# First block of a two-block transformer kernel: convolution rows stacked through HBM, two heads per root, router and its root with tokens on partitions, gates spread in one pass

## What is computed

```
h = rms_norm(x); z = h @ w_in            # 1024 -> 2304: a_val, a_gate, p_in, q, k, v
conv:  u = a_val * sigmoid(a_gate); 31-tap causal depthwise convolution of 256 channels;
       layer_norm, silu, @ w_pw (256 x 256)
pool:  causal means over 2, 4, 8, 16 tokens of 4 x 64 channels, minus the input, @ w_pool
attention: 4 heads, two score maps each, p0 - lam * p1, rms_norm of each head's output
x = x + concat(conv, pool, attention) @ w_out
hf = rms_norm(x); group logits hf @ wg (4) and expert logits hf @ we (16);
       best group, its 4 experts, top 2 of them -> gates (256 x 16)
y = sum over e of (silu(hf @ w_gate[e]) * (hf @ w_up[e]) * gates[:, e]) @ w_down[e]   # 16 experts, 256 wide
x = x + y
```

## Time and profile before

| | |
|---|---|
| median of 3 runs | 1813.24 us (1812.34 to 1813.38) |
| profiled execution, its own time | 1815.85 us |
| its span, first to last instruction | 1814.0 us |
| PE matmuls, share of the span | 1741.5 us, 96% |
| VectorE, ScalarE, GpSimd busy | 1196.5, 807.3, 271.7 us |
| mean granted TensorE clock | 0.983 of full |
| first block up to the experts' second turn | the first 195 us |

### The profile page before, as it was taken

One profiled execution on the slowest core, in us unless ns is written; L12 is line 12 of the kernel. 1 busy time (PEld: TensorE's weight loads), 2 busy tenths in 40 slices (PEclk: granted clock), 3 DMA queues, 4 the chain that ended last, 5 costly groups with the idle time before them and its releaser, 6 DMA issues.

```text
span 1814.0 us, 36961 instructions
## 1 busy us (share of the span) xinstructions
PE 1741.5 (96%) x13960; PEld 1668.6 (92%) x13960; DVE 1196.5 (66%) x2110; ACT 807.3 (45%) x1279; POOL 271.7 (15%) x270
## 2 busy tenths in 40 slices
PE   7697999999999999999999999999999899999996
PEld 7486999999999999888999999999999778999996
DVE  7366775676766566665787665766566566787755
ACT  4353443444444333444644443444433445554442
POOL 1022000001000110433240001000110333340012
PEclk9799899999999999999999999999999999999998
DMA  7223554555555554243445555555554342455553
GB/s 258 85 94 104 162 185 163 186 184 186 175 173 173 176 172 150 97 151 105 134 152 191 173 174 175 174 173 173 175 169 154 96 160 98 159 174 190 185 186 116
DMA packets 84038, 288.47 MB, mean 159 GB/s; under 512 B 9440, under 2 KB 16096, under 8 KB 83552
## 3 DMA queue, kind: packets, MB, share of 16 engines
q1 hardware_dynamic: 79584, 282.83, 47.2%
q10 hardware_dynamic: 4352, 4.20, 0.8%
HBM read 284.77 MB, written 1.05 MB: 158 GB/s over the span
## 4 chain that ended last, share of the span: by engine, by line
PE 87%; DVE 6%; ACT 3%; SPq 1%; issue 1%; POOL 1%; DMA 1%; ACTq 0%; POOLq 0%; DVEq 0%
PE PS L794 26%; PE PS L796 26%; PE PS L795 26%; DVE w_lo L1412 2%; PE PS L1284 1%; PE PS L1248 1%; ACT w_hi L430 1%; ACT S_all L670 1%; SPq L400 1%; PE PS L1288 1%; PE PS L1167 1%; PE PS L1256 1%; DVE x_lo L1417 0%; DMA h<-xT 0%; DVE PT L1991 0%
## 5 line engine op out<-in xcount | busy, mean ns | idle before, releaser
L1412 DVE TENSOR_TENSOR w_lo<-raw,w_hi 128x1024 fp32r<-128x1024 f32 x525 | 656.5, 1251 | 327.9 <-ACT w_hi L430 318.2
L794 PE MATMUL PS<-x_hi,w_hi 128*128 128x272 f32 (+1 forms) x2832 | 823.0, 291 | 16.0 <-DVE x_lo L1417 13.2
L796 PE MATMUL PS<-x_hi,w_lo 128*128 128x272 f32 (+1 forms) x2832 | 811.8, 287 | 0.0
L795 PE MATMUL PS<-x_lo,w_hi 128*128 128x272 f32 (+1 forms) x2832 | 810.1, 286 | 0.0
L430 ACT ACTIVATE w_hi<-raw 128x1024 fp32r<-128x1024 f32 x525 | 551.7, 1056 | 556.9 <-PE PS L796 550.9
L794 PEld LDWEIGHTS PS<-x_hi,w_hi 128*128 128x128 f32 x2832 | 537.3, 190 | 24.6 <-issue 18.9
L796 PEld LDWEIGHTS PS<-x_hi,w_lo 128*128 128x128 f32 x2832 | 537.6, 190 | 0.0
L795 PEld LDWEIGHTS PS<-x_lo,w_hi 128*128 128x128 f32 x2832 | 536.9, 190 | 0.7
L794 PE MATMUL PS<-a_hi,w_hi 128*128 128x272 f32 (+1 forms) x1280 | 366.2, 286 | 4.9 <-DVE a_lo L360 3.7
L796 PE MATMUL PS<-a_hi,w_lo 128*128 128x272 f32 (+1 forms) x1280 | 365.0, 285 | 0.0
L795 PE MATMUL PS<-a_lo,w_hi 128*128 128x272 f32 (+1 forms) x1280 | 364.4, 285 | 0.0
(11 more groups left out here) (270 smaller groups left out, 1258.4 us busy)
## 6 DMA issues: line engine op xcount, KB each, us to landing
raw<-stream SPq DMA_DIRECT2D x525, 512.0 KB, 3.3
biasB<-rpbz ACTq DMA_DIRECT2D x16, 256.0 KB, 3.2
G<-b1mats SPq DMA_DIRECT2D x2, 1024.0 KB, 7.6
h<-xT SPq DMA_DIRECT2D x1, 1088.0 KB, 7.7
out<-qk SPq DMA_DIRECT2D x8, 128.0 KB, 2.1
mat<-mats SPq DMA_DIRECT2D x1, 952.0 KB, 6.1
v_tok<-G SPq DMA_DIRECT2D x16, 35.5 KB, 1.9
mat<-G SPq DMA_DIRECT2D x16, 35.5 KB, 1.9
```

The lines of the kernel that those rows point to most:

```text
L794: pe.matmul(ps, hi, rh, start=first, stop=False)
L795: pe.matmul(ps, hi, rl, start=False, stop=False)
L796: return pe.matmul(ps, lo, rh, start=False, stop=last)
L1412: dve.tensor_tensor(w_lo[:, slot, :], raw[:, slot, :], w_hi[:, slot, :].bitcast(F32), ALU.subtract).then_inc(lo_done, 1)
```

## The change

1. SP stores each half of `U` once to an HBM tensor `u_rows` and loads each quarter of `U4[i]` from there in one DMA with an address pattern over all four groups: 2 stores and 8 loads for 32 copies. The loads of chunks 16 and 17 are placed around them. `conv()` and what follows it move one chunk later or more on every engine; `MISC` is reordered.
2. `o_norms(j)` takes the roots of two heads in one chain and scales them with one instruction.
3. `KEYS_A`, `KEYS_B` are reordered: heads 0 and 1 and the convolution first, pool and heads 2 and 3 last; the first chunk of the second part goes over two output tiles by pairs of input tiles.
4. The router's logits come with tokens on partitions. ScalarE squares h (`h_square`), GpSimd only adds; the mean square too comes with tokens on partitions, its root is a chain on 128x2, and PE spreads it (`rstd_spread`). `out1_tile` and `norm_lo` are interleaved so that `norm_lo` follows one tile later.
5. The two routing stages are one: `first_max` runs on the group logits and all four groups' expert logits together (10 rows of 4 for each token pair), twice for three times; then the gates, already times the root, are kept as two parts (16 rows each in 48), so that `gates_cast` is one fp32r matmul for each expert, and ScalarE copies the results (`gates_out`).

```diff
+        "spread2", "spread3", "v1", "pointwise"]
 MISC_AT = {e: i for i, e in enumerate(MISC)}
-B1_EVENTS = [("stat", 1), ("router", 0), ("router_turn", 0), ("gates_turn", 0)] + [("gates_cast", e) for e in range(8)]
+B1_EVENTS = [("router", 0), ("gates_turn", 0)] + [("gates_cast", e) for e in range(8)]
 B1E = {e: i for i, e in enumerate(B1_EVENTS)}
 B1_AUX = len(B1_EVENTS)
-TAPS, TAP_T = 8, 284
...
+            sp.wait_ge(conv_input, 1)
+            sp.dma_start(u_rows[0], U[:, 0, :]).then_inc(u_stored[0], 16)
+            reload(IN1 - 2, (IN1 - 2) % RING)
+            sp.wait_ge(conv_input, 2)
+            sp.dma_start(u_rows[1], U[:, 1, :]).then_inc(u_stored[1], 16)
             for i in range(2):
-                sp.wait_ge(conv_input, i + 1)
+                sp.wait_ge(u_stored[i], 16)
                 for s in range(4):
-                    for g in range(4):
-                        sp.dma_start(U4[i][32 * s:32 * s + 32, g, :], U[32 * g:32 * g + 32, i, s:s + TAP_T]).then_inc(taps_landed[i], 16)
+                    src = bass.AP(u_rows.tensor, i * P * UW_T + s, [[UW_T, 32], [32 * UW_T, 4], [1, TAP_T]])
+                    sp.dma_start(U4[i][32 * s:32 * s + 32, :, :], src).then_inc(taps_landed[i], 16)
+            reload(IN1 - 1, (IN1 - 1) % RING)
...
+                act.wait_ge(out_free, m + 1)
+                act.activation(squares[:, m, :], h[:, m, 0:SEQ], ACT.Square).then_inc(h_squared, 1)
...
                 if c == 18:
                     probs1_out(2)
+                    conv_mix_hi()
                     exp1(3)
...
+            for n in (IN1 + OUT1 + 2, IN1 + OUT1 + 3):
+                split_hi(n, n % RING)
...
+            act.wait_ge(rstd_spread, 1)
+            act.activation(rstd[:, 0:SEQ], PS[:, 7, 0:SEQ], ACT.Copy).then_inc(rstd_done, 1)
             act.wait_ge(router_centred, 1)
...
+            split_hi(IN1 + OUT1 + 4, (IN1 + OUT1 + 4) % RING)
+            act.wait_ge(aux_out, B1E["gates_turn", 0] + 1)
+            act.activation(gates_T, PS[0:48, 5, 0:SEQ], ACT.Copy).then_inc(gates_hi, 1)
+
+            def gates_out(half):
+
+                for e in range(4 * half, 4 * half + 4):
+                    k = B1E["gates_cast", e]
+                    act.wait_ge(aux_out, k + 1)
+                    act.activation(gates_bc[:, 2 * e:2 * e + 2, :], PS[:, 4 + k % 4, 0:512].rearrange("p (u t) -> p u t", u=2),
+                                   ACT.Copy).then_inc(aux_free, 1)
+
+            gates_out(0)
...
                     pv1(1)
-                if c == 10:
+                if c == 12:
+                    conv()
+                if c == 13:
                     o_turn(0)
-                if c == 11:
                     o_turn(1)
-                    conv()
-                if c == 12:
                     conv_mean()
-                if c == 13:
+                if c == 14:
                     conv_var()
-                if c == 14:
-                    conv_spread()
                     head_sums(1)
                 if c == 15:
+                    conv_spread()
                     head_spread(2)
+                if c == 16:
                     head_spread(3)
-                if c == 16:
-                    pointwise()
                     values_turn(1)
                     scores1(2)
                 if c == 17:
+                    pointwise()
                     scores1(3)
...
-                return pe.matmul(PS[0:20, 5, 0:SEQ], router_w[:, k, :], h[:, k, 0:SEQ], start=(k == 0), stop=(k == KD - 1))
+                for u in range(2):
+                    pe.matmul(PS[:, 4, 32 * u:32 * u + 20], h[:, k, u * P:(u + 1) * P], router_w[:, k, :],
+                              start=(k == 0 and u == 0), stop=(k == KD - 1), skip_group_check=True)
...
+            for j in range(KD // 2):
+                n = IN1 + 4 + j
+                pe.wait_ge(lo_done, n + 1)
+                order = [(m, x) for m in range(2) for x in range(4)]
+                if j == 0:
+                    order = [(m, x) for y in (0, 2) for m in range(2) for x in (y, y + 1)]
...
                 router(KD - 2)
-                aux_end(router(KD - 1))
+                router(KD - 1)
+                b = aux_begin()
+                pe.wait_ge(squares_summed, 2)
+                for u in range(2):
+                    pe.matmul(PS[:, b, 64 + 2 * u:66 + 2 * u], acc[:, u * P:(u + 1) * P], ones[:, 0:2], start=False, stop=False,
+                              skip_group_check=True)
+                pe.wait_ge(h_squared, KD)
+                for u in range(2):
+                    mm = pe.matmul(PS[:, b, 64 + 2 * u:66 + 2 * u], squares[:, KD - 1, u * P:(u + 1) * P], ones[:, 0:2],
+                                   start=False, stop=True, skip_group_check=True)
+                aux_end(mm)
...
+                if s == 1:
+                    pe.wait_ge(rs_ready, 1)
+                    for u in range(2):
+                        mm = pe.matmul(PS[:, 7, u * P:(u + 1) * P], router_cols(402 + u, 1).to_broadcast([P, P]), ident,
+                                       start=True, stop=True, skip_group_check=True)
...
+                    pe.wait_ge(gates_ready, 1)
+                    for u in range(2):
+                        mm = pe.transpose(PS[0:48, b, u * P:(u + 1) * P], router_cols(272 + 64 * u, 48), ident)
...
+                        mm = pe.matmul(PS[:, b, u * SEQ:(u + 1) * SEQ], gate_sel[:, 2 * e + u:2 * e + u + 1].to_broadcast([48, P]),
...
-            def o_norm(hd):
...
+            def o_norms(j):
+
+                dve.wait_ge(o_squared, 4 * j + 4)
+                s4 = o_ssq[:, 4 * j:4 * j + 4]
+                step(dve.tensor_scalar(s4, s4, 1.0 / (P * keep), EPS / keep, ALU.mult, ALU.add))
+                inverse_root(s4, o_rs[:, 4 * j:4 * j + 4], None, 0, root0[:, 0:4], root1[:, 0:4])
+                both = S_f[:, 1536:1536 + 2 * SEQ].rearrange("p (x t) -> p x t", x=4)
+                dve.tensor_tensor(both, both, o_rs[:, 4 * j:4 * j + 4].unsqueeze(2).to_broadcast([P, 4, P]), ALU.mult)\
+                   .then_inc(o_scaled, 1)
...
                 if c == 10:
-                    o_norm(0)
                     mix_heads(1)
-                if c == 11:
-                    o_norm(1)
+                if c == 12:
+                    o_norms(0)
+                if c == 14:
                     head_mix_lo(0)
-                if c == 12:
                     head_mix_lo(1)
-                if c == 13:
                     conv_centre()
-                if c == 14:
+                if c == 15:
                     conv_roots()
-                if c == 15:
-                    conv_scale()
                     head_roots(1)
                 if c == 16:
+                    conv_scale()
                     head_scale(2)
                     head_scale(3)
                 if c == 17:
                     logits(2)
-                    conv_mix_lo()
                 if c == 18:
                     logits(3)
                     denominators(2)
+                    conv_mix_lo()
                 if c == 19:
                     mix_heads(2)
                     denominators(3)
                 if c == 20:
-                    o_norm(2)
                     mix_heads(3)
                 if c == 21:
-                    o_norm(3)
-                    head_mix_lo(2)
+                    o_norms(1)
                     pool_mix_lo()
                 if c == 22:
+                    head_mix_lo(2)
                     head_mix_lo(3)
...
                 out1_tile(2 * j)
+                if j > 0:
+                    norm_lo(1, 2 * j - 1)
+                if j < 3:
+                    split_lo(c + AHEAD, (c + AHEAD) % RING)
+                out1_tile(2 * j + 1)
                 norm_lo(1, 2 * j)
-                split_lo(c + AHEAD, (c + AHEAD) % RING)
-                out1_tile(2 * j + 1)
-                norm_lo(1, 2 * j + 1)
-
-            split_lo(IN1 + OUT1 + AHEAD, (IN1 + OUT1 + AHEAD) % RING)
-            mean_square(1)
-
+            norm_lo(1, KD - 1)
...
+            step(dve.memset(router_cols(272, 128), 0.0))
             b = aux_bank()
-            dve.tensor_tensor(S_f[0:20, 0:SEQ], PS[0:20, b, 0:SEQ], rstd[0:20, 0:SEQ], ALU.mult).then_inc(aux_free, ax.up())
+            step(dve.tensor_scalar(ms_t.unsqueeze(2), PS[:, b, 64:68].rearrange("p (u x) -> p u x", u=2)[:, :, 0:1], 1.0 / D, EPS,
+                                   ALU.mult, ALU.add))
+            inverse_root(ms_t, rs_t, rs_ready, 1, t0_t, t1_t)
+            dve.wait_ge(rs_ready, 1)
+            step(dve.scalar_tensor_tensor(router_cols(0, 20), PS[:, b, 0:20], rs_t[:, 0:1], col[:, C_RB:C_RB + 20], ALU.mult, ALU.add))
+            dve.scalar_tensor_tensor(router_cols(20, 20), PS[:, b, 32:52], rs_t[:, 1:2], col[:, C_RB:C_RB + 20], ALU.mult, ALU.add)\
+               .then_inc(aux_free, ax.up())
...
+            first_max(LG, m1, o1)
+            dve.tensor_tensor(g_exp.unsqueeze(2), LGt[:, :, 0:1, :],
```

(30 more changed lines are left out.)

241 lines of the change are left out of this document (108 added, 133 removed).

## The result

The changed kernel takes **1780.18 us**, median of 4 runs (1778.10 to 1782.88), beside 1812.79 for the kernel before on the same chip (1812.31 to 1813.38): ratio 0.9817, 95% interval 0.9805 to 0.983, 32.6 us less. The forecast was 1778, the range 1770 to 1790. That is 1.9 more than the medians differ by, because the execution behind the earlier trace rows (1815.85) lies 3.1 above the median of its kernel and this one 1.2 above its own.

The account below looks back on a forecast made before the run. TensorE, busy 96% of the 1814.0 us span, bounds the kernel; time is won only where it waits or clocks low. Terms 21.9 - 3.0 + 16.7 = 35.6 give span 1778.4, median 1778, range 1770 to 1790.

Parts of the forecast that it names:

- Bound and unit: Whole kernel: TensorE busy 96% of 1814.0 us, time won only where it waits or clocks low; a matmul 0.116 us.
- Each wait and each run of narrow matmuls is followed by a stretch at 1.2 GHz: TensorE's clock: a wait therefore costs more than its own length; 1.7 us lost behind the x_lo wait.
- Part A: The convolution: 32.6 us from 60.2 to 92.79 become 10.7 us for the same work, gain 21.9 us.
- That, and no computation, made the 12.6 us of waits: Convolution: SP's issue of the copies, 10.09 us for 16, made TensorE's waits of 8.6 and 4.0 us.
- rival 1: Convolution: loads through HBM cost by rows, 2.5 us of SP each, 14 us less gain, 1791; chance 0.12.
- The rule of the Trainium skill: Convolution: throttled clock is the default, only recent activity lifts it; both halves may run at lower clock, 5.7 us worse.
- Part B: Between the convolution and w_out: old waits of 3.9 us against new costs of 6.9 us, loss 3.0 us.
- Part C: From w_out's second half to the experts' second turn: x_lo, gates, casts and clock, gain 16.7 us.
- a wait of 2.5 moves from chunk 30 to 31: Behind the first gate casts: TensorE's wait for a chunk's split only changes place, net gain 0.
- new falls: Router's end and casts: new places where the clock may fall, 1.7 us each, one and a half counted, -2.5 us.
- Behind 195 us only the second casts change, and products fill it.: Rest of the kernel behind 195 us: no other change expected when turning the span's sum into the median.
- 0.8 above the median by its span: Whole kernel: the traced execution's 1814.0 span against the 1813.24 median, so the forecast span 1778.4 became median 1777.6.

Follow-up runs that it names:

- experiment 1: Kernel before with chunk 17's reload behind the copies, loads through HBM, or both: 1808.79, 1803.97, 1798.18 us; changed kernel with the 32 copies back: 1792.14 us.
- mix_early: Changed kernel with conv_mix_hi ahead of probs1_out(2) on ScalarE and conv_mix_lo ahead of logits(3) and denominators(2) on VectorE: 1777.80 us, ratio 0.9789.
- after_again: The changed kernel run once more, nothing changed: 1779.88 us, ratio 0.9806 to the kernel before.
- before_hbm_behind: Kernel before with two stores and eight loads through HBM for the 32 copies, and chunk 17's reload issued behind them: 1798.18 us, ratio 0.9912.
- before_hbm: Kernel before with two stores and eight loads through HBM for the 32 copies, at the same place in SP's list: 1803.97 us, ratio 0.9947.

## Why the prediction was right, point by point

- **Bound and unit.** Right in the main: the gain lies in the first 260 us, in TensorE's waits and its lower clock, and beside them in less work, which the bound leaves out and the sum has: at full clock eight casts went from 3.79 to 1.20, 2.6 less, twice. "Each wait and each run of narrow matmuls is followed by a stretch at 1.2 GHz" was too strong: in the trace of before, the clock stays full behind the wait that ends at 61.87 and behind the 16 matmuls of two columns at 103.61.
- **Part A: size right (21.9; 22.5), the account of it incomplete.** The step "That, and no computation, made the 12.6 us of waits" is the one that failed. SP's issue was one cause, the reload of chunk 17 ahead of the copies another: 4.9 us alone (experiment 1). The sum was not hurt, because it began at 59.8 and the diff moves the reload too. A load took 0.47 us of SP, not 0.63; rival 1's 2.5 is excluded. Chunk 13 was to start near 72.9 and started at 71.9, in a trace that runs 1.0 ahead. `L1031` has no wait and its 128 records take 7.04 us (64.86 to 71.90; 7.0 forecast) at a clock of 1.00. The rule of the Trainium skill ("TensorE: Matmul & The Clock Gate", "The HAM clock gate") that I weighed against the change did not bite: no matmul of the convolution ran at the lower clock.
- **Part B: sum right (-3.0; -3.3), made of other terms.** The wait at chunk 18 was 3.2, not 2.5, with the clock behind it as said (0.72 over 6 us); `mix_early` shows its cause to be the place of `conv_mix`. But the sum followed VectorE's list (`logits(3)`, `denominators(2)`), and ScalarE's `conv_mix_hi` came later than that by 0.8. The joint root cost `o_turn(2)` 0.7, not 1.0, the low part behind it 0.2, not 0.5. `head_spread(2)` waited 1.1 in `after_again` (1.2 forecast) and no time that the first trace lists, where the clock had fallen at 82 and chunk 15 took 4.6 us in place of 3.1; this fall was not in the sum.
- **Part C: too low by 2.7 (16.7; 19.4).** `x_lo` with its clock: 4.2 forecast; chunk 26 starts 20.4 ahead (157.50, 137.09) and chunk 27 24.6 ahead (166.30, about 141.7). The gates: one wait of 3.9 became two of 0.16 and 1.18, 1.3 in place of my 1.5. Casts 1.19 and 1.20 for 1.1 twice. The term mis-sized is "a wait of 2.5 moves from chunk 30 to 31": in this execution it was 0.9, because chunk 30 ran at the lower clock and covered the rest; in `after_again`, where chunk 30 ran at full clock, it was the 2.5 of the text. That is 1.6 of the 2.7; and of the new falls, counted at 2.5, there was one in this part, 1.7 (0.57 over 4 us).
- **"Behind 195 us only the second casts change, and products fill it."** True of the work, false of the time: 4.1 us went where the clock fell in code that nobody had touched, four places against two in the kernel before, and 0.9 in the last 60 us. This is what brought the lead of 39.5 down to 34.5, 1.1 short of the 35.6 that was forecast. Part C's error and this one have opposite signs, so the close sum is in part luck; without the second the time would have been near 1775.
- **From the sum to the median.** The medians differ by 32.6, 3.0 less than the sum, and 1.9 of this is the choice of trace. "0.8 above the median by its span" set a span beside a time: by its own time that execution lay 2.6 above the 1813.24. It lost 1.5 us to the lower clock at 1556, which none of the three variants of the kernel before in experiment 1 has in its trace; whether this is the usual case for that kernel is open, as it has one trace.

## What to carry to other kernels

When a DMA is late, read what its queue did ahead of it before counting what it costs: here a reload held ready data for 5 to 8 us, and moving it gave 4.9 us without any new path. Of a forecast that moves all later work, say that unchanged narrow work or waits further on may meet the lower clock or not; compare two variants by the lead that each has at a marked instruction, and take their spans only for what is larger than two such stretches. Part of a wait that is removed can be handed to the next late step, as from chunk 18 to chunk 31 here, so try the two edits together before judging either.

## What the runs showed that I had not expected

- A store of 144 KB to HBM landed in 1.9 us (median; 1.7 and 2.1) in the changed kernel, where the first left 3.5 us and the second 1.7 us behind a reload, in 3.0 in `before_hbm_behind`, and in 3.9 in `before_hbm`, right behind a reload of 512 KB. The Trainium skill, "DMA: Bandwidth & Descriptors", "Anatomy of one DMA", gives about 2 us of fixed cost for a transfer issued by GpSimd; these were issued by SP, and the 1.9 is near it, the 3.9 is not.
- 20 matmuls of 10 rows in 2.51 us were followed by the lower clock in two traces of the same kernel and by the full one in the kernel before, with TensorE busy throughout; one such stretch costs 1.5 us.
- The eight 32-bit casts of 256 columns cost 3.7 to 3.8 us at full clock with 48 rows as with 16, and 1.2 in fp32r.
